# A two-layer decoder trunk in split fp32: the order of token tiles at the sub-layer boundaries, and a ring shared by raw weights and low parts

## The reference

```
c_act = silu(c)
for i in range(2):
    mod = c_act @ ada_w[i] + ada_b[i]                     # 1024 x 6144, a row vector
    sh1, sc1, g1, sh2, sc2, g2 = split(mod, 6)
    h = rms_norm(x, norm_mix[i]) * (1 + sc1) + sh1
    y = dilated_attention(h, ...) if i == 0 else hgrn2_mixer(h, ...)
    x = x + g1 * y
    h = rms_norm(x, norm_ffn[i]) * (1 + sc2) + sh2
    x = x + g2 * ((silu(h @ w1[i]) * (h @ w3[i])) @ w2[i])      # hidden width 2816
return x
```

## Time and profile before

| what | value |
|---|---|
| median of 3 runs | 909.22 us (908.17 to 912.74) |
| span of the profiled execution | 910.1 us; this is also the time that is known of it |
| TensorE, VectorE, ScalarE, GpSimd busy | 847.7, 623.6, 426.3, 119.3 us |
| units split and rounded | 126 |
| moved by DMA | 188.96 MB, 208 GB/s in the mean |

### The profile page before, as it was taken

The page is one execution under the profiler, slowest core; times in us unless marked ns, Lnnn a source line. Parts: engine busy times, 40 slices in busy tenths (PEclk is TensorE's granted clock), DMA queues, the critical chain, the costliest instruction groups (busy, mean ns, idle before and its releaser), DMA issues.

```text
span 910.1 us, 10752 instructions
## 1 busy us (share of the span) xinstructions
PE 847.7 (93%) x4195; PEld 709.3 (78%) x4195; DVE 623.6 (69%) x749; ACT 426.3 (47%) x515; POOL 119.3 (13%) x159
## 2 busy tenths in 40 slices
PE   1599999999999979999999979999989799999997
PEld 0477888889888858888888857888877588888886
DVE  5879678677686767766777775895774754454543
ACT  3255446545455355333433446658554553433431
POOL 4101001010010010111111100462620000000000
PEclk9999999999999999999999979999979899999999
DMA  9899766876767627889889835444224175555541
GB/s 339 284 271 310 240 224 214 274 222 231 230 221 243 190 89 249 286 277 316 283 278 318 294 109 182 139 139 139 93 93 139 46 225 191 185 185 185 185 139 46
DMA packets 119607, 188.96 MB, mean 208 GB/s; under 512 B 5580, under 2 KB 90758, under 8 KB 119558
## 3 DMA queue, kind: packets, MB, share of 16 engines
q1 hardware_dynamic: 105350, 137.90, 47.4%
q0 software_dynamic: 14208, 50.39, 15.9%
HBM read 187.18 MB, written 1.09 MB: 207 GB/s over the span
## 4 chain that ended last, share of the span: by engine, by line
PE 81%; DVE 8%; DMA 4%; ACT 3%; issue 2%; SPq 2%; DVEq 0%; ACTq 0%
PE bank L390 69%; PE bank L659 2%; PE bank L508 2%; PE bank L484 2%; DMA raw<-in_attn_w_qkv_dram 1%; DVE wlo L1052 1%; PE bank L469 1%; PE bank L604 1%; ACT arena L774 1%; PE bank L434 1%; SPq L268 1%; PE bank L406 1%; DMA arena<-in_distance_table_dram 1%; DMA bias_rows<-arena 1%; DMA ada_w<-in_ada_w_dram 1%
## 5 line engine op out<-in xcount | busy, mean ns | idle before, releaser
L1052 DVE TENSOR_TENSOR wlo<-raw,whi 128x2048 fp32r<-128x2048 f32 x126 | 288.7, 2291 | 126.6 <-ACT whi L724 126.3
L390 PE MATMUL bank<-whi,hT_hi 128*128 128x512 f32 (+1 forms) x800 | 315.7, 395 | 8.7 <-DVE hT_lo L1145 8.3
L724 ACT ACTIVATE whi<-raw 128x2048 fp32r<-128x2048 f32 x126 | 241.5, 1916 | 150.3 <-PE bank L390 120.5
L390 PE MATMUL bank<-whi,hT_lo 128*128 128x512 f32 (+1 forms) x800 | 308.5, 386 | 0.0
L390 PE MATMUL bank<-wlo,hT_hi 128*128 128x512 f32 (+1 forms) x800 | 308.0, 385 | 0.0
L390 PEld LDWEIGHTS bank<-whi,hT_hi 128*128 128x128 f32 x800 | 152.7, 191 | 42.6 <-DVE hT_lo L1145 10.1
L390 PEld LDWEIGHTS bank<-whi,hT_lo 128*128 128x128 f32 x800 | 152.4, 191 | 30.4
L390 PEld LDWEIGHTS bank<-wlo,hT_hi 128*128 128x128 f32 x800 | 152.8, 191 | 28.8 <-issue 1.0
L1077 DVE SCALAR_TENSOR_TENSOR acc<-ada_w,cact,acc 128x1024 f32<-128x1024 f32 x80 | 102.3, 1279 | 25.0 <-DMA ada_w<-in_ada_w_dram 24.6
L390 PE MATMUL bank<-whi,oT_hi 128*128 128x512 f32 x240 | 97.4, 406 | 3.6 <-DVE oT_lo L1430 1.6
L312 POOL DMA_DIRECT2D ada_w<-in_ada_w_dram x80 | 42.6, 532 | 408.3 <-DVE acc L1077 408.3
(11 more groups left out here) (137 smaller groups left out, 734.0 us busy)
## 6 DMA issues: line engine op xcount, KB each, us to landing
raw<-in_ffn_w_dram SPq DMA_DIRECT2D x88, 512.0 KB, 4.9
ada_w<-in_ada_w_dram POOLq DMA_DIRECT2D x80, 512.0 KB, 5.2
raw<-in_attn_w_qkv_dram SPq DMA_DIRECT2D x64, 512.0 KB, 4.8
raw<-in_ffn_w_dram SPq DMA_DIRECT2D x22, 1024.0 KB, 6.0
raw<-in_hgrn_w_in_dram SPq DMA_DIRECT2D x16, 1024.0 KB, 5.4
arena<-in_ada_w_dram POOLq DMA_DIRECT2D x16, 512.0 KB, 6.6
raw<-in_attn_w_qkv_dram SPq DMA_DIRECT2D x4, 1024.0 KB, 5.1
raw<-in_attn_w_out_dram SPq DMA_DIRECT2D x4, 1024.0 KB, 6.0
```

The lines of the kernel that those rows point to most:

```text
L390: mm = nc.tensor.matmul(d[:, 0:n], l, r[:, k, cut], start=first and k == 0 and q == 0, stop=last and k == nk - 1 and q == 2)
L724: return nc.scalar.activation(dst, src, ACT.Copy)
L1052: nc.vector.tensor_tensor(wlo[:, m % SPL, :], raw[:, m % RAW, :], fp(whi[:, m % SPL, :]), ALU.subtract).then_inc(s["split"], 1)
```

## The change

1. `raw` and `wlo` share one ring of six units (`RAW` = 6) at the same addresses; `split_unit` writes the low part over the raw weights. `whi` has four slots (`SPL` = 4). A load of unit m (m >= 6) waits for `pe_unit` of m - 6; loads 3 to 5 wait for the splits as before.
2. Three units per sub-layer have their high part in a spare part of `arena` (`spare_hi`).
3. At the end of each sub-layer the last units (two to three, `TRIPLE` = 3 in the FFN) do token tile 0 in all of them, then tile 1. `first_units` does three units: tile 0 of all, then tile 1. `norm_t(q, 0)` moves into the last tile, `norm_t(q, 1)` into tile 0 of the third unit.
4. The late heads are renumbered (both tiles 0 first), three of them run together, with other banks.
5. The adaLN operations are dealt out anew: two instead of one in units 3 to 6, 32 in steps 5 to 29 of the first FFN, 8 in steps 3 to 18 of the second. Three gate reductions leave the boundaries.
6. `hidT` has four slots, the last hidden block uses other banks, the masks are loaded in two parts, the output goes out in four pieces, and in the last three units of the program tile 1 is done by column block.

```diff
-RAW = 3
-SPL = 3
+RAW = 6
+SPL = 4
+PREFETCH = 3
+TRIPLE = 3
...
+        raw = nc.alloc_sbuf_tensor_at("raw", [P, RAW, UNIT], F32, offset=ring_at)
+        wlo = nc.alloc_sbuf_tensor_at("wlo", [P, RAW, UNIT], F32R, offset=ring_at)
...
+        spare_hi = {M_FFN0 + 1: ..., M_IN + 1: ..., M_FFN1 + 1: ...}
+        def hi_of(m):
+            return spare_hi[m][:, :] if m in spare_hi else whi[:, m % SPL, :]
...
+                if PREFETCH <= m < RAW:
+                    sp.wait_ge(s["split"], m - PREFETCH + 1)
                 if m >= RAW:
-                    sp.wait_ge(s["split"], m - RAW + 1)
+                    sp.wait_ge(s["pe_unit"], m - RAW + 1)
...
-                sp.dma_start(masks[:], a["pair_masks"]).then_inc(s["masks_in"], 16)
+                sp.dma_start(diagonal[:], a["pair_masks"][:, 0:P]).then_inc(s["masks_in"], 16)
...
     first_units:
+                    unit(m + 2, hT_hi, hT_lo, 4, 0, 512, third, True, False, tiles=(0,), ks=(0, 1))
+                    norm_t(q, 1)
+                    unit(m + 2, hT_hi, hT_lo, 4, 0, 512, third, False, False, tiles=(0,), ks=(2, 3))
...
     late heads, TensorE:
+            out_tile(3, 0, tile_done="y_first")
+            out_tile(1, 1)
+            att_transposes(LATE + 3)
+            pe.wait_ge(s["ot_ev"], LATE + 3)
             out_tile(2, 1)
+            att_values(LATE + 3)
+            norm_t(1, 0)
+            pe.wait_ge(s["ot_ev"], LATE + 4)
+            out_tile(3, 1)
...
     FFN, TensorE, the last three units:
+                for j in last:
+                    pe.wait_ge(s["f_lo"], NF * f + j + 1)
+                    last_unit(j, 0, tile_done="y_first" if j == NF - 1 else None)
+                    if j == NF - TRIPLE:
+                        hidden_transposes(f, NF - 1)
+                if f == 0:
+                    for j in last[:-1]:
+                        last_unit(j, 1)
+                    last_unit(NF - 1, 1, ks=(0,))
+                    norm_t(2, 0)
+                    last_unit(NF - 1, 1, ks=(1,))
...
     recurrence output, TensorE:
+            mixed_tile(2, 0)
+            mixed_tile(3, 0, tile_done="y_first")
+            mixed_tile(2, 1)
+            mixed_tile(3, 1, ks=(0,))
+            norm_t(3, 0)
+            mixed_tile(3, 1, ks=(1,))
...
     round_unit, ScalarE:
                 if m >= SPL:
                     act.wait_ge(s["pe_unit"], m - SPL + 1)
-                copy(whi[:, m % SPL, :], raw[:, m % RAW, :]).then_inc(s["rounded"], 1)
+                copy(hi_of(m), raw[:, m % RAW, :]).then_inc(s["rounded"], 1)
...
     late heads, ScalarE:
+            round_unit(M_FFN0 + 1)
+            norm_stats(1, 0)
             att_evac(LATE + 3)
...
     after the first FFN, ScalarE:
+            round_unit(M_IN + 1)
             norm_stats(2, 0)
...
     boundary, VectorE:
-                residual(q - 1, last_unit, range(3))
+                residual(q - 1, base - 1, range(2))
                 norm_scale(q, 0)
+                if late_head:
+                    att_out(LATE + 3)
                 norm_affine(q, 0)
                 norm_rest(q, 0)
+                residual(q - 1, base - 1, range(2, 4))
+                split_unit(base + 2)
                 norm_scale(q, 1)
...
     before boundary(2), VectorE:
+            split_unit(M_IN + 1)
+            boundary(2, M_IN)
...
+def ada_done(m):
+    return 2 * KC + m + 1 + min(max(m - 2, 0), 4)
```

More of the change, by code:

```diff
@@ L278, in _ @@
                         load_bias(sp, h)
[L279 to L282, removed]
+            for b in range(2 * T):
+                t, c = divmod(b, 2)
+                sp.wait_ge(s["res"], 4 * 3 + b + 1)
+                sp.dma_start(out[0, t * P:(t + 1) * P, c * 512:(c + 1) * 512], x[:, t, c * 512:(c + 1) * 512]
+                             ).then_inc(s["out_done"], 16)
+            sp.wait_ge(s["out_done"], 16 * 2 * T)
         @block.gpsimd
@@ L313, in _ @@
                                ).then_inc(ada_in[n % ADA_RING], 16)
+            for n in range(ADA_FFN1):
+                ada_load(n)
             def rec_diff(half, level):
@@ L336, in _ @@
                     rec_diff(half, level)
+            pool.wait_ge(s["r_q"], 2 * LEVELS)
+            pool.wait_ge(s["r_mm"], 2 * PRODUCTS)
+            for n in range(ADA_FFN1, 2 * ADA_BLOCKS * KC):
+                ada_load(n)
         PURE = PAIRS * QU
@@ L376, in _, with unit @@
         @block.tensor
         def _(pe):
-            def unit(m, lhs_hi, lhs_lo, nk, k0, n, dst, first, last, tiles=range(T), tile_done=None):
-                sl = m % SPL
-                w = [v[:, sl, :].rearrange("p (k n) -> p k n", k=nk) for v in (whi, wlo)]
+            def unit(m, lhs_hi, lhs_lo, nk, k0, n, dst, first, last, tiles=range(T), tile_done=None, ks=None,
+                     cols=None, block_done=None):
+                w = [v.rearrange("p (k n) -> p k n", k=nk) for v in (hi_of(m), wlo[:, m % RAW, :])]
@@ L541, in _ @@
             out_tile(0, 0)
-            att_scores(LATE)
-            att_scores(LATE + 1)
+            for J in range(LATE, LATE + 3):
+                att_scores(J)
+            pe.wait_ge(s["v_ev"], 2 * PAIRS)
             out_tile(0, 1)
@@ L546, in _ @@
             out_tile(1, 0)
-            att_transposes(LATE)
-            att_transposes(LATE + 1)
-            out_tile(1, 1)
+            for J in range(LATE, LATE + 3):
+                att_transposes(J)
+            pe.wait_ge(s["ot_ev"], 12)
+            out_tile(2, 0, ks=(0,))
             att_values(LATE)
             att_values(LATE + 1)
-            att_scores(LATE + 2)
+            out_tile(2, 0, ks=(1,))
+            att_values(LATE + 2)
             att_scores(LATE + 3)
-            pe.wait_ge(s["ot_ev"], 12)
@@ L574, in ffn @@
                     n = NF * f + j
[L575 to L587, removed]
@@ L1016, in _ @@
                         rec_exp(half, o - 1)
-                round_unit(M_IN + step + AHEAD)
+                if step:
+                    round_unit(M_IN + step + AHEAD)
                 if step == 9:
@@ L1037, in _ @@
                 rec_out_round(1, t)
-            round_unit(M_OUT1 + 2 + AHEAD)
-            round_unit(M_OUT1 + 3 + AHEAD)
+            round_unit(M_FFN1)
+            act.wait_ge(s["r_q"], 2 * LEVELS)
+            round_unit(M_FFN1 + 1)
+            norm_stats(3, 0)
             ffn(1, M_FFN1)
@@ L1051, in split_unit @@
                 dve.wait_ge(s["rounded"], m + 1)
-                nc.vector.tensor_tensor(wlo[:, m % SPL, :], raw[:, m % RAW, :], fp(whi[:, m % SPL, :]), ALU.subtract
+                nc.vector.tensor_tensor(wlo[:, m % RAW, :], raw[:, m % RAW, :], fp(hi_of(m)), ALU.subtract
                                         ).then_inc(s["split"], 1)
@@ L1278, in qkv_extra @@
                     att_max(J)
-                ada_op(2 * KC + m)
+                for n in range(ada_done(m - 1), ada_done(m)):
+                    ada_op(n)
                 if pr >= 1 and j % 2 == 0 and j < 8:
@@ L1514, in base_of @@
     f, j = divmod(n, NF)
[L1515 removed]
+    return (M_FFN0, M_FFN1)[f] + (3 * (j + 1) + 1 if j < NF - TRIPLE else 2 * NF + j)
 _INS = ["x", "c", "rel_bias", "ada_w", "ada_b", "norm_mix", "norm_ffn", "attn_w_qkv", "attn_w_out", "attn_q_gain",
```

361 lines of the change are left out of this document (203 added, 158 removed).

## The result

The changed kernel takes 930.62 us (median of 4 runs, 928.98 to 931.64), the kernel before 908.69 beside it: ratio 1.024, 95% interval 1.0215 to 1.0257. It is 2.4% slower. I had forecast 911.1 with a range of 902 to 918, so the time lies outside the range.

What follows compares the result with a forecast made beforehand. TensorE, busy 93% of the span, was taken as the bound. Start -6.3, boundaries 0, -1.2 and +4.0, end +1.6 sum to 1.9 us longer: 912.0 - 0.9 = 911.1 us, range 902 to 918.

Steps and rivals of the forecast that it cites:

- The start: Units 3 to 6: doubled ada operations wait for their loads and delay qk_normalise; 6.3 us lost, from -12.5 to -2.
- The two waits: At the start, TensorE waits for qk_normalise(1) and qk_normalise(2): 3.5 and 3.8 us, together 7.3.
- an earlier unit 3: At the start, a smaller mask load lets unit 3 arrive perhaps 1.0 us earlier (0 to 1.85).
- One rival: Ada loads keep up, clock holds at the two long waits: 903.5 us, or 902.6 with 3.2 us landings; chance 0.28.
- L: Landing time of an ada load at the start, taken as 6.2 us; 3.2 by a documentation page's rule.
- Boundary 1: Late heads and start of the first FFN: 10.0 us of waits and lower clock before and after, gain 0.
- Boundary 2: Before norm_t(2, 0): a new wait of 6.1 us, 11.4 us against 10.2 today, so 1.2 us lost.
- the reading of `round_unit`: At boundaries 1 and 2, roundings into spare buffers still wait for `pe_unit`, giving waits of 6.3 and 6.1 us.
- Boundary 3: Before norm_t(3, 0) and the second FFN: waits of 5.2 us against 9.2 today, so 4.0 us gained.
- The end: After the last matmul: one block instead of two gains 1.4 us, a smaller last output piece 0.2; gain 1.6.
- The pace of the matmuls: All units: 72 matmuls take 16.35 us, one token tile of a unit 2.73 us; no change counted.
- The rival of late loads: At the start, ada loads land at 7.5 us or later: start -11.5, time 916.3 us; chance 0.20.

Runs made afterwards that it cites:

- the run without the needless wait: Changed kernel, with the rounding into a spare buffer waiting for one unit less: 919.25 us, ratio 1.0102 to the kernel before.
- Undone alone: Changed kernel with the four extra early ada operations spread to units 12, 18, 24 and 30: 925.36 us, 5.3 us less than 930.62.
- done alone in the kernel before: Kernel before with two ada operations in units 3 to 6 and none at the late heads: 915.19 us, 6.5 us more.
- both variants of the kernel before: Kernel before with first-FFN reductions ahead of their units, 921.48 us; kernel before with two ada operations in units 3 to 6, 915.19 us.
- the first experiment: Changed kernel with the four first-FFN reductions of steps 12, 18, 19 and 24 put back behind their units: 915.36 us, ratio 1.0064.
- all three edits: Changed kernel with reductions behind their units, ada operations spread, and spare-buffer roundings without the extra wait: 898.67 us, ratio 0.9888; timed again 902.11 us, 0.9913.

## Why the prediction was wrong, step by step

- **The start, -6.3 forecast.** The mechanism is right and the size near: +6.7 at group 10 from -0.7, less the two gate reductions that the changed kernel has done by then (1.7), so 5.7 us; 3.4 us at the lower clock cost 1.7 of them. The two waits were to be new at 3.5 and 3.8 us; the trace has 4.2 at the first and nothing at the second. There the load issued at 90.75 us landed after 4.15 us instead of 6.2, and TensorE itself came 1.7 us later by its lower clock. That is chance in part: the profile of the run without the needless wait, whose start is the same, has 3.99 and 3.62 us. At group 39, where both have done the same reductions, -0.7 has become +4.3: 5.0 us lost, against a forecast of 7.3. The 1.0 us that an earlier unit 3 was to bring did not come: the wait of 1.85 us that it was to remove was still 1.60. The 0.7 us of group 0 lie ahead of it and are not explained. Undone alone: 5.3 us; done alone in the kernel before: 6.5 us. One rival's sum was wrong: with L = 3.2 the formula has no wait at all, so the start would be +1.0 and not -0.2, and that time 901.4 and not 902.6.

These rows are VectorE at the start of the changed kernel: start, us, instruction, [idle before]. They are two pairs of operations; the second operation of each waits for its load, 1.81 and 1.64 us, and the first not at all or 0.42 us.

```profile
70.47 1.28 DVE L1182 SCALAR_TENSOR_TENSOR acc<-ada_w,cact,acc 128x1024 f32<-128x1024 f32 x1
73.56 1.28 DVE L1182 SCALAR_TENSOR_TENSOR acc<-ada_w,cact,acc 128x1024 f32<-128x1024 f32 x1 [1.81 <-DMA ada_w<-in_ada_w_dram]
...
78.59 1.28 DVE L1182 SCALAR_TENSOR_TENSOR acc<-ada_w,cact,acc 128x1024 f32<-128x1024 f32 x1 [0.42 <-DMA ada_w<-in_ada_w_dram]
81.52 1.28 DVE L1182 SCALAR_TENSOR_TENSOR acc<-ada_w,cact,acc 128x1024 f32<-128x1024 f32 x1 [1.64 <-DMA ada_w<-in_ada_w_dram]
```

- **Boundary 1, 0 forecast.** From group 39 to 47 +4.3 becomes +2.4, so 1.9; by then the changed kernel has yet to do one reduction (0.86) and four hidden transposes (0.44), so +0.6 is gained. The wait of 6.3 us was 6.11, the 0.5 behind it did not come, 1.5 was 1.46.
- **Boundary 2, -1.2 forecast.** +21.4 to +22.7, and two reductions less (1.7), so -3.0. The wait of 6.1 us was 6.10. The wait behind the transposes was 0.98 and not 2.5 us. Not in the forecast was a second spell at the lower clock, from 584.2 us on: in the two spells TensorE was busy for 6.3 us, which is an estimate of 3.2 us lost where I had added 1.0. A wait of 0.95 us for the low part of the last hidden block, where I had counted on the cover of one tile, lies ahead of group 76 and counts to the first FFN. The run without the needless wait shows that the reading of `round_unit` was right: 11.4 us for both boundaries.
- **Boundary 3, +4.0 forecast.** +21.8 to +16.6, so +5.2. The waits 1.9, 1.5, 1.5 were 1.90, 1.47, 1.46, and the clock stayed up, 1.00 where it had been 0.79. The forecast sum was 5.2 us of waits; the trace has 4.8, which leaves 0.8 of the 5.2 us gain unexplained.

```profile
728.94 1.09 PE L464 MATMUL bank<-ident,arena 128*128 128x128 f32 x8 [1.90 <-DVE arena L1231]
732.87 0.50 PE L446 MATMUL bank<-whi,hT_hi 128*128 128x512 f32 x1 [1.47 <-DVE hT_lo L1249]
743.81 0.50 PE L446 MATMUL bank<-whi,hT_hi 128*128 128x512 f32 x1 [1.46 <-DVE hT_lo L1249]
```

- **The end, +1.6 forecast.** 0.8: the last add ends 1.4 us behind the last matmul as forecast (924.15 to 925.56), but from there to the end of the span it takes 3.6 us, where it was 3.1. In the other runs it is 3.1 us in both variants of the kernel before and 2.4 to 3.6 in those of the changed kernel, so what half the bytes bring is lost in this scatter.
- **The pace of the matmuls, 0 forecast.** The prediction priced every unit with the 2.73 us per tile of the kernel before. In every trace of the kernel before and of its two variants 72 matmuls without a wait take 16.35 us; in every trace of the changed kernel and its variants 16.51 or 16.52, with the clock at 1.00 and so also where both were timed on one chip. One row of each in the second FFN:

```profile
778.51 16.35 PE bank L390 x72
...
778.50 16.51 PE bank L446 x72
```

Some 2600 matmuls follow one another in this way, on average 229.2 ns apart where it was 227.3: an estimate of 5.0 us in the whole program. Why the same matmuls follow one another more slowly in the new program was not tested.
- **What failed.** Two sentences: that the reductions "stand in the waits today and become real work elsewhere", so that they cancel, and that in the feed-forward units "TensorE waited for none" of the ada operations. I counted a reduction as 0.86 to 1.68 us of work and did not ask, for a step that was moved, what it waits for and where that stands on VectorE. The two programs show what changed: the place, from behind the unit to ahead of it, and the steps, from 8, 14, 15 and 20 to 12, 18, 19 and 24. Two neighbouring steps for one block were there before, but step 14 had no gate product and step 18 has one. The price is 15.3 us by the first experiment, against 19.1 us in the spans; with it the sum of the prediction would have been 926, and with the pace 931. That this comes so near to 930.62 is luck in part: the errors of the other five terms, in the order above +1.3, +0.6, -1.8, +1.2 and -0.8 (measured less forecast gain), nearly cancel. The rival of late loads named the right resource (load, operation, TensorE) in the wrong stage: two of the three waits hang on a load that landed 5.7 us after its issue.

What is left: the second FFN loses 3.3 us from group 101 to 129. Two gate reductions that moved there are 2 x 0.86 of it, and the other 1.6 us are the pace, 28 groups of 0.055 us. The first FFN loses 19.0 us from group 47 to 76. Of this 1.3 are the reduction and the transposes still to be done at group 47, and 14.9 lie in groups 60 to 70. Of the other 2.8 us the pace is an estimate of 1.0 and the wait for the last hidden block 0.95; the last 0.9 are open.

## What to carry to other kernels

When an instruction moves on one engine, write down each semaphore that it waits for and the place of the instruction that raises it on its own engine; a step of slack between two programs is none when the second engine is itself led by the first. A ring of two with a load per operation allows two operations per (landing + operation + issue), here 6.2 + 1.3 + 0.3 = 7.8 us; a unit takes 5.5 us, so two operations per unit make the ring the bound while VectorE stands idle ahead of them. Before a sum is trusted, compare the pace of undisturbed work in both profiles too. And a spare buffer takes a wait away only if the wait in the code is taken away too.

## What the runs showed of the hardware

- The clock of TensorE fell behind waits of 1.95 us (24 matmuls took 6.87 us, 5.47 is usual) and did not behind one of 1.90 us and two near 1.46 us at boundary 3. The wait of 1.85 us at the start of the kernel before left the clock at 1.00; one of 1.83 us at the same place, in the second profile of all three edits, was followed by 3.4 us at the lower clock. So two waits of the same length may differ by over 1 us in what follows, and the prediction's assumption that waits under 2 us leave the clock up does not hold.
- With two ada loads under way at once the landings in 60 to 98 us were 3.8, 5.9 and 6.8 us (least, median, most), not longer than the 5.4, 6.7 and 7.5 us with mostly one:

```profile
DMA to landing us min/median/max: 3.8/5.9/6.8
```

- Reading the raw weights and writing the low part over them takes 2296 ns; with separate places it was 2291.
- All three edits take most of the time at the lower clock away: PEclk is 0.994 in the mean over the whole span (0.992 in the second profile), 0.978 in the changed kernel. By these means 41 us at the lower level become 11, so at most an estimated 15 of the 32 us gained; it is less, because TensorE is idle in part of that time.
- The pace of matmuls that wait for nothing differs between two programs with the same matmuls at a granted clock of 1.00: 72 take 16.35 us in one and 16.51 in the other, in every trace.
